# Expert rows by one-hot products instead of gathers: two transformer blocks with a mixture of experts on one core

## The chip, the cores and the metric

The kernel runs on one core of a Trainium2 chip. The metric is the device time of one execution in microseconds (us). A core has TensorE (PE, matmuls; its weight loads are listed as PEld), VectorE (DVE), ScalarE (ACT), GpSimd (POOL) and SyncE (SP), each with its own instruction queue, and 16 DMA engines that all queues share. The queues wait for each other on semaphores only. SBUF is the memory of 128 partitions on the core, PSUM the eight banks (2 KB for each partition) that TensorE writes to, HBM (DRAM) the memory outside.

## The reference, cut to what matters

A first pair of blocks (attention variants and convolution FFNs) feeds a second pair, whose mixers are a latent attention (layer 0) and a short convolution (layer 1). Each layer of the second pair ends in a mixture of experts on 256 tokens of width 1024, all in float32:

```python
g_prob = jax.nn.softmax(hf @ w_group, axis=-1)                 # 4 groups
g_sel = jnp.argmax(g_prob + b_group, axis=-1)
e_prob = jax.nn.softmax(chosen group's 8 logits)               # 32 experts in all
_, top_idx = lax.top_k(e_prob + e_bias, 2)                     # 2 experts of that group
top_w = top_w / sum(top_w) * g_w
y[token] = sum over its 2 experts: w * (silu(x @ w_gate[e]) * (x @ w_up[e])) @ w_down[e]
x = x + g2 * y
```

That is 512 assignments of a token to an expert in each layer. An expert's three matrices (1024 x 512, 1024 x 512, 512 x 1024) are 6.29 MB, so the 32 experts of a layer are 201 MB.

## The kernel before, in words

**Routing.** VectorE and TensorE work out for each token its two experts and a slot for each assignment. Slots are cut into 48 blocks (`NB`) of 32 slots; each block belongs to one expert, every expert has at least one block, and the blocks that no expert needs are spread over the experts by share (`rest`, `pad_i`). Three blocks make a round, so there are 16 rounds (`ROUNDS`) of 96 slots (`ROWS`). The end of the routing (`route`, L2331 to L2366) makes from the slot numbers `dst_f` two one-hot factors (`onA`, `onB`), multiplies them on TensorE, and reads off for each slot of each round the token (`token_i`), the row in which its result goes (`yrow_i`) and its weight (`slot_w`). `tab_i` tells each engine which of three buffers a block's expert lies in and how many loads must have landed; `need_i` tells SP when a buffer is free.

**Rows of a round.** ScalarE stores the normalized tokens `fN` to `f_rows` in DRAM (L1730, L1735). POOL gathers the 96 rows of a round from there into `xe` by an indirect DMA (L2764); indices of empty slots are out of bounds and are skipped. TensorE turns `xe` (eight transposes, L1208), ScalarE copies them out of PSUM into `xeT` (L1665).

**A round** (`turn` on TensorE and VectorE, the loop over `b` on ScalarE). Eight quarters of gate and up products, then four of down products, each with three column tiles of 32 columns on TensorE at once, one for each block (L1216 twice, L1218 once). One block's weights are read where they were loaded; those of the two others are first copied quarter by quarter into `side`, by VectorE (L2400) and ScalarE (L1684). VectorE's `landed` and `tail_landed` wait for the loads at quarters 0 and 2 of each matrix and tell ScalarE (`half_landed`). ScalarE's silu (L1672) and VectorE's product with `slot_w` (L2421) give `hm`; four transposes (L1245) and two copies (L2427) turn it, and the down products follow. VectorE multiplies the result by the gate row `gb2` into `ym` (`rows_out`, L2408, after the second copy of the next round), and POOL scatters `ym` to `y_rows` in DRAM by an indirect DMA (L2775). TensorE and VectorE run their rounds in hardware loops, so VectorE reads its four values of `tab_i` at the start of each round (L2412, L2413).

**Weights.** SP loads the experts in order into the three buffers, in half-matrices of 1 MB (`load_experts`, L767): gate of expert e, down of e-1, up of e. Each half waits until the rounds that use the old expert in that buffer are done with it (`need_i` against `quarter_done`). The first three experts are loaded before the rounds.

**After the rounds.** SP reads `y_rows` back (L812), two contributions to each token, and VectorE adds them to the residual (`combine`, L2448, L2449). For layer 1, VectorE (`row_diags`, L2213), TensorE (`row_pair`, two products of 128x128 by 128x512 a pair) and ScalarE (L1656) then spread three gate rows over the partitions. Squares (L1565), a root, transposes and the convolution's products (L843) follow in layer 0; the closing norm and the store follow in layer 1.

## Time and profile before

| what | value |
|---|---|
| time, 3 runs | median 2247.94 us (2244.13 to 2252.44) |
| the profiled execution | time 2246.04 us, span 2244.2 us |
| mean granted TensorE clock | 0.932 of full |
| rounds of layer 0 | first products at 1066.5 us, last result written at 1555.4 us |
| rounds of layer 1 | first products at 1730.6 us, last result written at 2220.8 us |

The span is the time between the first and the last record of the profiled execution; its own time has 1.8 us more around it. Times inside the profile are counted from the span's start. Busy shares are those of an engine's own instructions; an engine that waits for a semaphore is idle.

### The profile page before, as it was taken

The page shows a single profiled execution, that of the slowest core. Times are in us where ns is not written, and L with a number is a line of the kernel's source. Part 1 is how long each engine was busy: PE and PEld are TensorE (multiplying, and loading weights), DVE is VectorE, ACT ScalarE, POOL GpSimd, SP SyncE. Part 2 cuts the span into 40 slices and gives each one's busy share as a digit, 9 for nine tenths or more (in the row PEclk, how much of TensorE's full clock was granted, in tenths as well). Part 3 has the DMA queues.
Part 4 walks back from the last instruction along what each step waited for, and adds up shares of the span by engine and source line. Part 5 has one row for each costly group of instructions (what it writes and reads, how often), then busy time and mean ns, then how long its engine had stood idle before and what let it go on. Part 6 is the DMA issues. An engine that isn't in the chain of part 4 may idle for free.

```text
span 2244.2 us, 29502 instructions
## 1 busy us (share of the span) xinstructions
PE 1929.4 (86%) x9453; PEld 1085.2 (48%) x9454; DVE 956.4 (43%) x2077; ACT 665.8 (30%) x1053; POOL 100.0 (4%) x133
## 2 busy tenths in 40 slices
PE   8878999999999999997976887777897967877885
PEld 4534777745577775554432433333764423323332
DVE  2273888312478534444432432334224423323333
ACT  1142000012400002132543543444102534434443
POOL 2000000000000000000000000000000000000000
PEclk9869999999899999998998998999997988888998
DMA  8502898433179543305899999996645999999994
GB/s 282 201 6 99 325 343 312 178 141 143 66 277 358 197 167 132 124 31 207 334 421 383 360 412 407 407 416 260 258 160 221 385 421 379 415 421 389 411 394 166
DMA packets 84611, 617.69 MB, mean 275 GB/s; under 512 B 16289, under 2 KB 16609, under 8 KB 21809
## 3 DMA queue, kind: packets, MB, share of 16 engines
q1 hardware_dynamic: 68912, 544.70, 61.3%
q0 software_dynamic: 14752, 69.77, 8.3%
q10 hardware_dynamic: 864, 2.19, 0.2%
q8 instruction: 44, 0.72, 0.1%
q14 instruction: 39, 0.31, 0.0%
HBM read 621.84 MB, written 19.92 MB: 286 GB/s over the span
## 4 chain that ended last, share of the span: by engine, by line
PE 67%; DMA 19%; DVE 5%; issue 3%; ACT 3%; DVEq 2%; SPq 1%; ACTq 0%; POOLq 0%
PE ps L843 25%; PE ps L1216 15%; PE ps L1053 14%; DMA big<-in_w_up 7%; PE ps L1065 7%; DMA big<-in_w_down 5%; DMA big<-in_w_gate 5%; PE ps L1218 3%; PE ps L857 2%; ACT big L1684 2%; DVEq L2413 1%; DVE hT L2421 1%; PE ps L1245 1%; DMA c_res<-f_rows,big 1%; PE ps L1208 1%
## 5 line engine op out<-in xcount | busy, mean ns | idle before, releaser
L1216 PE MATMUL ps<-big,hT 128*32 128x512 f32 x3072 | 723.5, 627 | 144.0 <-ACT big L1684 140.5
L1218 PE MATMUL ps<-big,hT 128*32 x1536 | 722.3, 627 | 0.0
L1684 ACT COPY big<-big 128x1024 f32 x384 | 395.0, 1046 | 526.2 <-PE ps L1218 267.1
L2400 DVE TENSOR_SCALAR big<-big 128x1024 f32 x384 | 263.0, 696 | 623.0 <-PE ps L1218 375.6
L1216 PEld LDWEIGHTS ps<-big,hT 128*32 128x32 f32 x3072 | 200.5, 114 | 541.3 <-DVE big L2400 276.0
L1053 PE MATMUL ps<-hT,big 128*128 128x256 f32 x1408 | 311.1, 379 | 0.0
L843 PE MATMUL ps<-big,hT 128*128 128x512 f32 (+4 forms) x792 | 299.7, 537 | 4.8 <-DMA big<-in_dense 2.5
L1053 PEld LDWEIGHTS ps<-hT,big 128*128 128x128 f32 x1408 | 266.7, 190 | 49.0 <-issue 14.8
L843 PEld LDWEIGHTS ps<-big,hT 128*128 128x128 f32 x792 | 144.4, 195 | 149.3 <-issue 139.7
L843 PE MATMUL ps<-big 64*30 64x256 f32 (+14 forms) x704 | 161.4, 512 | 30.7 <-DVE big L2350 8.3
L1218 PEld LDWEIGHTS ps<-big,hT 128*32 128x32 f32 x1536 | 164.8, 114 | 6.1 <-issue 0.9
L1065 PE MATMUL ps<-big 128*128 128x512 f32 x352 | 159.2, 595 | 0.4 <-DVE big L2163 0.4
L2173 DVE SCALAR_TENSOR_TENSOR big<-big,s_ccol 128x512 f32<-128x512 f32 x196 | 147.4, 752 | 7.0
L1648 ACT ACTIVATE big<-big 128x256 f32<-128x256 f32 x44 | 18.3, 417 | 363.8 <-DVE big L2155 363.8
L843 PEld LDWEIGHTS ps<-big 64*128 64x128 f32 (+8 forms) x704 | 81.7, 196 | 90.3 <-issue 63.1
L843 PE MATMUL ps<-hT,big 128*128 128x256 f32 (+1 forms) x480 | 112.8, 398 | 1.9 <-ACT hT L1897 1.9
L843 PEld LDWEIGHTS ps<-hT,big 128*128 128x128 f32 x480 | 92.4, 193 | 22.7 <-issue 10.7
L1065 PEld LDWEIGHTS ps<-big 128*128 128x128 f32 x352 | 66.1, 190 | 72.9 <-issue 69.0
L2137 DVE TENSOR_TENSOR big<-ps,big 128x512 f32<-128x512 f32 x44 | 30.4, 690 | 119.5 <-PE ps L1053 117.5
L1245 PE MATMUL ps<-c_ident,hT 96*128 96x96 f32 x128 | 29.5, 318 | 50.4 <-DVE hT L2421 50.4
L857 PE MATMUL ps<-c_ident,big 128*128 128x128 f32 (+4 forms) x349 | 57.4, 301 | 17.6 <-DVE big L2085 10.9
L2764 POOL DMA_INDIRECT c_res<-f_rows,big x32 | 32.5, 1014 | 715.4 <-PE ps L1208 486.7
(333 smaller groups left out, 1176.2 us busy)
## 6 DMA issues: line engine op xcount, KB each, us to landing
big<-in_w_down SPq DMA_DIRECT2D x128, 1024.0 KB
big<-in_w_gate SPq DMA_DIRECT2D x128, 1024.0 KB, 12.1
big<-in_w_up SPq DMA_DIRECT2D x128, 1024.0 KB, 12.9
big<-in_dense SPq DMA_DIRECT2D x52, 1536.0 KB, 8.3
big<-in_dense POOLq DMA_DIRECT2D x28, 2048.0 KB, 9.9
big<-in_dense SPq DMA_DIRECT2D x21, 2048.0 KB, 8.3
big<-in_dense SPq DMA_DIRECT2D x5, 1024.0 KB, 7.5
big<-y_rows SPq DMA_DIRECT2D x4, 1024.0 KB, 6.2
```

The lines of the kernel that those rows point to most:

```text
L843: ins = nc.tensor.matmul(out, lhsT, rhs, start=start, stop=stop)
L857: ins = nc.tensor.transpose(out, rows, const["ident"][0:k, 0:k])
L1053: ins = nc.tensor.matmul(ps[:, t % 2, f * S:(f + 1) * S], w[:, k, f * P:(f + 1) * P], hT[:, k, S:2 * S], start=k == 0, stop=k == KT - 1)
L1065: ins = nc.tensor.matmul(ps[:, 4 + 2 * c + h, :], gT[:, t % 2, c * P:(c + 1) * P], w[:, h * BW:(h + 1) * BW], start=t == 0, stop=t == FT - 1)
L1216: nc.tensor.matmul(ps[g * SLOTS:(g + 1) * SLOTS, bank, :], xT[:, k, g * SLOTS:(g + 1) * SLOTS], side[:, g - 1, quarter % 2, at:at + BW], s ...
L1218: return nc.tensor.matmul(ps[0:SLOTS, bank, :], xT[:, k, 0:SLOTS], experts3[:, bass.ds(here, 1), kind * CH + row:kind * CH + row + BW] .re ...
L1245: ins = nc.tensor.transpose(ps[:, 4 + 3 * h, k * ROWS:(k + 1) * ROWS], rows, const["ident"][0:ROWS, 0:ROWS])
L1684: nc.scalar.copy(side[:, 1, quarter % 2, :], experts3[:, bass.ds(there, 1), lo:lo + QW] .rearrange("p a n -> p (a n)")).then_inc(s["side2_ ...
L2137: tt(U[:, par, :, 2:S + 2], ps[:, par, :].rearrange("p (a b) -> p a b", a=2), token_scale, mult)\
L2173: ins = stt(acc, mod_w[j % 2][:, k, :], ccols[:, k, col:col + 1], acc, mult, add)
L2400: ts(side[:, 0, quarter % 2, :], experts3[:, bass.ds(there, 1), lo:lo + QW].rearrange("p a n -> p (a n)"), 1.0, None, mult).then_inc(s["si ...
L2764: nc.gpsimd.indirect_dma_start(out=xe, out_offset=None, in_=f_rows[:, :], in_offset=bass.IndirectOffsetOnAxis(ap=token_i[:, b:b + 1], axis=0),
```

## The change

It rewrites how a round gets its rows and gives its results back, and moves some work around it.

- **Rows by products.** `fN` stays in SBUF. VectorE writes for each round a one-hot matrix of tokens by slots (`first_pick`, `second_pick`: two `tensor_scalar` and two `scalar_tensor_tensor` of 128x96), and TensorE multiplies it with the tokens (`rows_of`: two banks, each two float32 products of 128x96 by 128x512). ScalarE and VectorE copy one half each out of PSUM into `xe` (`row_half`), and the eight transposes (`rows_T`) follow, now between the second and the third quarter of the down products of the round before. `f_rows`, its stores and the gathers are gone.
- **Results in slot order.** The slot weight is no longer multiplied into `hm`. ScalarE stores all 96 rows of `ym` to their place in `y_rows` by a plain DMA on its own queue (`store`, after the fourth copy of the next round). While the last round runs, POOL fetches each token's two rows by four indirect DMAs (`fetch`), and VectorE adds them with the token's weight. The last round's results are not stored: a weighted one-hot matrix (`last_picks`, `turn_last`, `hot`) spreads them by four products, and VectorE adds these last. The rows of the last round in `y_rows` are zeroed once, by two DMAs on POOL in the first FFN.
- **VectorE's rounds unrolled.** The values of the next round's `tab_i` are read in the middle of the round, two before the copies of the turned hidden rows and two after them. The ninth copy comes ahead of those copies too.
- **Routing.** The products of `onA` and `onB` and what leads to them are gone; `past` is made earlier, from a reduction, and `row_half` of round 0 stands ahead of `need_i` and `tab_i`. TensorE and ScalarE wait for the end of the routing only after round 0's transposes.
- **Layer 1's gate rows** are spread during the first three steps of the convolution, which has six PSUM banks in place of eight.

The spreading of the spare blocks, the loads of weights and their order are as before. The diff, cut to its core:

```diff
-                pe.wait_ge(g2["act_evac"].sem, g2["act_evac"].end)
-                for q in range(2 * TC):
-                    mm(ps[:, 6, 0:3 * ROUNDS], onA[:, q, :], onB[:, q, :, :], q == 0, q == 2 * TC - 1,
...
-                def rows_T(b, h, first=False):
-                    if h == 0:
-                        pe.wait_ge(s["rows_gathered"].sem, s["rows_gathered"].at(b * 16 + 16))
...
+                def rows_of(b, first=False):
+
+                    pe.wait_ge(s["pick_ready"].sem, s["pick_ready"].at(b * TC + TC))
...
+                    for h in range(2):
+                        for t in range(T):
+                            ins = nc.tensor.matmul(ps[0:ROWS, h, :], onehot[:, t, :], fN[:, t, h * BW:(h + 1) * BW],
+                                                   start=t == 0, stop=t == T - 1)
+                        ins.then_inc(s["rows_ready"].sem, 1)
...
+                def rows_T(b):
+
...
+                    for h in range(2):
+                        for k in range(4):
+                            rows = xe[0:ROWS, :].rearrange("t (p k) -> t k p", k=KT)[:, 4 * h + k, :]
+                            ins = nc.tensor.transpose(ps[:, h, k * ROWS:(k + 1) * ROWS], rows,
...
+                    if more:
+                        rows_of(b + 1)
+                    else:
+                        turn_last()
                     for h in range(2):
-                        if more:
-                            rows_T(b + 1, h)
...
                     for k in range(FFK):
+                        if k == 2 and more:
+                            rows_T(b + 1)
...
-                rows_T(0, 0, first=True)
-                rows_T(0, 1, first=True)
+                rows_of(0, first=True)
+                rows_T(0)
+                after(pe, "ent" + name[-1], "route" + name[-1], "g2_" + name[-1])
...
+                for c in range(T):
+                    for h in range(2):
+                        if c == 0:
+                            pe.wait_ge(m["last_ready"].sem, m["last_ready"].at(h + 1))
+                        mm(ps[:, 2 * c + h, :], hot[0:ROWS, c, :], ym[0:ROWS, h * BW:(h + 1) * BW], True, True,
...
+                if t < 3:
+                    if t:
+                        g = st["g1_1"]["gate_copied"]
+                        pe.wait_ge(g.sem, g.at(2 * t))
+                    row_pair("g1_1", t, CONV_BANKS)
...
+                def store(b):
+                    act.wait_ge(s["y_ready"].sem, s["y_ready"].at(b + 1))
+                    act.dma_start(rows[b * ROWS:(b + 1) * ROWS, :], ym[0:ROWS, :]).then_inc(s["y_stored"].sem, 16)
...
+                row_half(0)
+                rows_T(0)
+                after(act, "route" + name[-1])
                 there = third(0)
...
-                    for j in range(2, 6):
+                    for j in range(2, 4):
+                        copy(b, there, j)
+                    if b:
+                        store(b - 1)
+                    for j in range(4, 6):
...
+                    here = there
+                    if b + 1 < ROUNDS:
+                        row_half(b + 1)
+                        there = third(b + 1)
+                    for j in range(10, 12):
+                        copy(b, here, j)
...
-                act.wait_ge(e["z_done"].sem, e["z_done"].end)
-                act.dma_start(f_rows[0:P, :], fN[:, 0, :]).then_inc(e["f_stored"].sem, 16)
...
-                L(nc.vector.tensor_copy(dst_i, dst_f))
...
-                L(tt(onA, iota(4, P), wide(q_f, P), ALU.is_equal))
-                for x in range(3):
-                    ins = tt(onB[:, :, x, :], eqB, wide(vals[:, :, x], ROUNDS), mult)
...
+                L(stt(rel, iota(4, ROUNDS), -float(ROWS), wide(dst_f, ROUNDS), mult, add))
+                m = st["moe" + tag]
+                first_pick(m, 0)
+                second_pick(m, 0)
+                row_half(m, 0)
+                nc.vector.tensor_copy(row_i, dst_f)
...
+            def first_pick(s, b):
+
+                for t in range(TC):
+                    ts(onehot[:, t, :], const["iota"][:, 0:ROWS], rel[:, t, b:b + 1], None, ALU.is_equal)\
...
+                for t in range(TC):
+                    v.wait_ge(s["pick_step"].sem, s["pick_step"].at(b * TC + (t + 1)))
+                    stt(onehot[:, t, :], const["iota"][:, 0:ROWS], rel[:, TC + t, b:b + 1], onehot[:, t, :],
...
-                def turn(b, first=False, second=False):
-                    there = v.value_load(tab_i[0:1, 0, bass.ds(b * WIDE + 1, 1)], min_val=0, max_val=BPE - 1)
...
-                            rows_out(b - 1, second)
+                            rows_out(b - 1)
+                        if j == 3 and not last:
+                            v.wait_ge(s["rows_ready"].sem, s["rows_ready"].at(b * 2 + 2))
+                            first_pick(s, b + 1)
+                        if j == 4 and not last:
+                            second_pick(s, b + 1)
+                        if j == 4 and last:
+                            last_picks()
...
-                    stt(hm[0:ROWS, :], sgm[0:ROWS, :], slot_w[0:ROWS, bass.ds(b, 1)], ps[0:ROWS, 3, :], mult, mult)\
-                        .then_inc(s["hidden_done"].sem, 1)
+                    tt(hm[0:ROWS, :], sgm[0:ROWS, :], ps[0:ROWS, 3, :], mult).then_inc(s["hidden_done"].sem, 1)
+                    copy(b, there, loads, 9, first)
+                    if not last:
+                        then, ahead = second(b + 1), [loads_of(b + 1, 0)]
...
+                    if not last:
+                        row_half(s, b + 1)
+                        ahead += [loads_of(b + 1, q) for q in range(1, BPE)]
+                        following = then, ahead
...
-                turn(0, True)
-                after(v, "g2_" + name[-1])
-                turn(1, False, True)
-                with v.Fori(2, ROUNDS) as b:
-                    turn(b)
...
+                values = second(0), [loads_of(0, q) for q in range(BPE)]
+                for b in range(ROUNDS):
...
+                    values = turn(b, *values)
+                v.wait_ge(m["last_turned"].sem, m["last_turned"].end)
+                nc.vector.tensor_copy(hot[0:ROWS, :, :], ps[0:ROWS, 0, 0:T * P].rearrange("p (c n) -> p c n", c=T))\
...
                 for c in range(T):
-                    v.wait_ge(s[f"y_fetched_{c}"].sem, s[f"y_fetched_{c}"].end)
-                    for h in range(2):
-                        cols = slice(h * BW, (h + 1) * BW)
...
-                        link(v, tt(out, out, y01[:, c, 0, cols], add))
-                        tt(out, out, y01[:, c, 1, cols], add).then_inc(s["combined"].sem, 1)
+                    v.wait_ge(m[f"y_fetched_{c}"].sem, m[f"y_fetched_{c}"].end)
+                    for k in range(2):
+                        link(v, stt(lat(c), y01[c][:, k, :], tok_w[:, k * T + c:k * T + c + 1], lat(c), mult, add))
...
+                for h in range(2):
+                    cols = slice(h * BW, (h + 1) * BW)
+                    tt(ym[0:ROWS, cols], ps[0:ROWS, 5 + h, :], gb2[0:ROWS, 0, cols], mult).then_inc(m["last_ready"].sem, 1)
+                for i, (out, c, h) in enumerate(parts):
+                    v.wait_ge(m["last_spread"].sem, m["last_spread"].at(i + 1))
+                    tt(out, out, ps[:, 2 * c + h, :], add).then_inc(m["combined"].sem, 1)
...
+            row_diags("g1_1", 1)
...
-                    nc.gpsimd.indirect_dma_start(
-                        out=xe, out_offset=None, in_=f_rows[:, :],
-                        in_offset=bass.IndirectOffsetOnAxis(ap=token_i[:, b:b + 1], axis=0),
-                        bounds_check=S - 1, oob_is_err=False).then_inc(s["rows_gathered"].sem, 16)
...
-                    nc.gpsimd.indirect_dma_start(
-                        out=y_rows[:, :], out_offset=bass.IndirectOffsetOnAxis(ap=yrow_i[:, b:b + 1], axis=0),
-                        in_=ym, in_offset=None, bounds_check=2 * S - 1, oob_is_err=False)\
...
+                        nc.gpsimd.indirect_dma_start(
+                            out=y01[c][:, k, :], out_offset=None, in_=y_rows[layer][:, :],
+                            in_offset=bass.IndirectOffsetOnAxis(ap=row_i[:, q:q + 1], axis=0),
...
+                pool.dma_start(y_rows[l][(ROUNDS - 1) * ROWS:ROUNDS * ROWS, :], zeros[0:ROWS, :])\
```

## Rows read from the trace of the kernel before

**Rows 1.** The page: GB/s moved in each of 40 slices.
```profile
GB/s 282 201 6 99 325 343 312 178 141 143 66 277 358 197 167 132 124 31 207 334 421 383 360 412 407 407 416 260 258 160 221 385 421 379 415 421 389 411 394 166
```

**Rows 2.** Stretches: length, busy time and count by engine; TensorE clock, DMA share, GB/s.
```profile
1071.70:1100.00 28.30, 26.36 (x182) 12.07 (x179) 12.03 (x18) 17.09 (x18) 2.01 (x2) 1.00 0.89 329
1100.00:1540.00 440.00, 347.50 (x2204) 153.70 (x2201) 149.22 (x226) 193.17 (x213) 27.70 (x27) 0.93 0.99 402
...
1577.80:1662.70 84.90, 84.88 (x384) 74.10 (x384) 16.24 (x39) 8.00 (x15) 0.00 (x0) 0.98 0.57 217
...
1760.00:2195.00 435.00, 344.01 (x2173) 150.72 (x2167) 146.00 (x221) 189.60 (x208) 27.13 (x27) 0.91 1.00 405
...
1278.00:1290.00 12.00, 11.13 (x78) 5.83 (x81) 6.19 (x9) 7.81 (x9) 1.01 (x1) 1.00 0.57 190
```

**Rows 3.** Groups by line in layer 0's rounds: busy us, mean ns, idle before them.
```profile
L1216 PE MATMUL ps<-big,hT 128*32 128x512 f32 x1536 | 361.1, 625 | 70.0 <-ACT big L1684 69.6 <-DVE hT L2427 0.3
...
L1208 PE MATMUL ps<-c_ident,c_res 96*128 96x96 f32 x126 | 21.2, 296 | 0.0
...
L1245 PE MATMUL ps<-c_ident,hT 96*128 96x96 f32 x64 | 14.7, 317 | 27.3 <-DVE hT L2421 27.3
```

**Rows 4.** Timeline (start, us): two rows_out, and the first product between rounds.
```profile
1093.08 1.21 DVE L2408 TENSOR_TENSOR c_res<-ps,hT 96x1024 f32<-96x1024 f32 x1
...
1117.67 1.21 DVE L2408 TENSOR_TENSOR c_res<-ps,hT 96x1024 f32<-96x1024 f32 x1
...
1117.47 0.62 PE L1216 MATMUL ps<-big,hT 128*32 128x512 f32 x2 [1.35 <-ACT big L1684]
```

**Rows 5.** Timeline of SP and TensorE in a later round: two issues of down weights, one wait.
```profile
1231.39 0.92 SPq L767 DMA_DIRECT2D big<-in_w_down  x2
...
1262.66 0.84 SPq L767 DMA_DIRECT2D big<-in_w_down  x2
...
1243.10 0.48 PE L1245 MATMUL ps<-c_ident,hT 96*128 96x96 f32 x2 [3.53 <-DVE hT L2421]
```

**Rows 6.** Chain that ended last, two pieces of the down products behind that wait.
```profile
1245.55 0.85 PE ps L1216 x2
...
1248.01 0.42 PE ps L1216 x2
```

**Rows 7.** Timeline of POOL, DVE and PE at the start of layer 0's rounds.
```profile
1056.10 1.06 POOL L2764 DMA_INDIRECT c_res<-f_rows,big  x1 [49.73 <-DVE big L2366]
...
1059.68 0.69 DVE L2400 TENSOR_SCALAR big<-big 128x1024 f32 x1 [3.62 <-issue]
...
1063.40 1.51 PE L1208 MATMUL ps<-c_ident,c_res 96*128 96x96 f32 x8 [7.79 <-DMA c_res<-f_rows,big]
...
1066.52 1.07 PE L1216 MATMUL ps<-big,hT 128*32 128x512 f32 x2 [1.60 <-ACT big L1684]
```

**Rows 8.** Chain: eight records of a 128x512 product, four float32 products, at full clock.
```profile
1026.19 3.44 PE ps L843 x8
```

**Rows 9.** One line, 1100 to 1540 us: DVE's loads of table values, min/median/max ns.
```profile
L2413 DVEq TENSOR_LOAD <-big x42: 297/304/324, 1113.8 to 1525.7; - x42
```

**Rows 10.** Timeline: last rows_out and last square, of layer 0 and of layer 1.
```profile
1554.14 1.22 DVE L2408 TENSOR_TENSOR c_res<-ps,hT 96x1024 f32<-96x1024 f32 x1 [2.63 <-PE ps L1218]
...
1572.51 0.19 ACT L1565 ACTIVATION_READ_ACCUMULATOR big<-x_res 128x1 f32 x1
...
2219.53 1.22 DVE L2408 TENSOR_TENSOR c_res<-ps,hT 96x1024 f32<-96x1024 f32 x1 [2.63 <-PE ps L1218]
...
2236.91 0.19 ACT L1565 ACTIVATION_READ_ACCUMULATOR big<-x_res 128x1 f32 x1
```

**Rows 11.** Groups by form: a product-and-add of 128x1024 and an addition of 128x512.
```profile
L2449 DVE TENSOR_TENSOR x_res<-x_res,big 128x512 f32<-128x512 f32 x8 | 5.5, 692 | 0.3
...
L2244 DVE SCALAR_TENSOR_TENSOR big<-x_res,rstd_x,c_res 128x1024 f32<-128x1024 f32 x2 | 2.6, 1277 | 0.0
```

**Rows 12.** One tensor, y_rows: DMAs from issue to landing, us.
```profile
DMA to landing us min/median/max: 3.1/8.2/9.1
```

288 lines of the change are left out of this document (146 added, 142 removed).

## The prediction, made before the changed kernel ran

> **What bounds the kernel now.** I read the slices of the page first [rows 1]. The two stretches near 400 GB/s are the rounds of the experts, 2 x 490 us of 2244, and all but a few edits lie in them or at their ends. The highest slice is 421 GB/s; I take it as the rate of a full stream. The stretches [rows 2] then show how near to it the rounds are: 402 and 405 GB/s, with TensorE busy 79% of the time. So the weights' stream nearly sets the pace: two experts a round, 12.58 MB, plus 0.26 MB of gathered and scattered rows (only the 512 real ones of a layer move) is 12.84 MB, or 30.5 us at 421. But the stream has holes: 1071.7 to 1100 at 329, and 1278 to 1290 at 190 GB/s [rows 2]. In each layer they are worth some 25 us, and who makes them decides this change.
>
> Three kinds of round can be told apart.
> - *TensorE sets it.* Two results stand 24.6 us apart [rows 4]. That is 48 groups of 0.43 us (two records of L1216 a group, 1536 in 16 rounds [rows 3]), so 20.6, and 4.0 of turning rows, waits and a gap of 1.35 at the round's start, where the side copies wait for VectorE, which reads its table there [rows 4].
> - *A loop sets it.* Two issues of down weights stand 31.3 us apart [rows 5]. A down load can't be issued until the gate products of its round let the gate load ahead of it in SP's queue go; VectorE's ninth copy waits for the landing, and the hidden product is behind that copy in VectorE's queue. TensorE stands idle for 3.53 us in front of the hidden transposes [rows 5]. Of the 16 waits in layer 0, which sum to 27.3 [rows 3], 7 are of 2.7 to 3.6 us; layer 1 has 6 of 2.5 to 3.6.
> - *The stream sets it*: the rest, 8 in each layer.
>
> **Part 1, the pick products and where they stand.** A round gets four float32 products of 512 columns, 3.44 us at full clock [rows 8], after the up products. Its eight transposes were 1.3 us beside them (21.2 for 126 [rows 3]) and are now 1.4 inside the down products. VectorE's ninth copy (0.69) and two table reads come ahead of the copies of the turned hidden rows. A read's load alone takes 0.30 us [rows 9]; four reads with the landing waits took 3.62 [rows 7]; I take 0.5 a read (0.3 to 0.9). The gap at the round's start goes, as the table is read early.
>
> In a round that TensorE sets: 3.44 hides the hidden product, the copy and the reads; the down products start 4.4 us after the last up product in place of 2.15, so +2.2; transposes +1.4; gap -1.4; sum +2.2 us, 26.8 in all. I count one such round in layer 0 whose length reaches the end (the one in front of the hole at 1278), and in layer 1 two, one of them half covered: +2.2 and +3.3. The first three rounds are as long, but three experts were there before them and the stream runs full behind them: their lengthening costs only the first down load's release, +1.0 in each layer (0 to 2.2).
>
> In a loop round the products stand in the 3.53 us in which TensorE waits for the down weights to land, so they cost nothing; without that wait they would cost 2.2 as above. After the wait: the copy and the reads ahead, less the four transposes that leave, +0.7; transposes +1.4; gap -1.5; and TensorE's clock. The four groups behind the wait took 0.85 to 1.0 us and the later ones 0.42 [rows 6]: the lower level of 1.2 GHz, then 2.4. With the products in the wait the idle time is under 1.7 us, shorter than waits after which groups of full speed stand in this trace, so -1.7. Sum -1.1 (+0.6 if the clock still falls). But each round now stores all 96 rows, 0.39 MB in place of 0.26, so the stream's own floor is 12.98 MB, 30.8 us. From 31.3 to 30.8 is -0.5: 7 rounds -3.5, 6 rounds -3.0. Bounds: +0.6 and -0.5 a round.
>
> In a stream round the 0.13 MB costs 0.3 us: +2.4 in each layer (0 if the store fills holes).
>
> **Part 2, the start of the rounds.** Now: the gather starts at 1056.1, the transposes at 1063.4, the first product at 1066.5 [rows 7]. After: `dst_f` is ready near 1051.0 (five tiny operations ahead of the picks, 0.2 each, in place of seven and two products), picks 1052.1. The four products take 3.44 at full clock or 6.88 at the lower level, at which the first group at 1066.5 ran (1.07 [rows 7]); I take 5.5, near the colder end, as the clock recovered 2.9 us into that work: 1057.6. Half row copy 0.7, need and table 1.2, VectorE's reads and landing waits 3.6 as before, ScalarE's side copy 1.05: 1064.3. So -2.2 in each layer (-4.3 to -0.8). POOL and ScalarE lose their gather and two stores here; nobody waited for those stores.
>
> **Part 3, the end.** From the last down product (0.1 us ahead of `rows_out`) to the last square: 1572.7 less 1554.0 is 18.7 us in layer 0, and 2237.1 less 2219.4 is 17.7 in layer 1 [rows 10]. After it, counted from that product: VectorE is free 2.7 us before it; `hot` and the gains to -1.9; four `scalar_tensor_tensor` of 1024 columns at 1.28 plus 0.03 [rows 11] to +3.3; two halves of the gated result at 0.65 to +4.6. TensorE has idled 4 us by the first half, so I take its first two products at 1.72 (the lower level) and the others between: 5.8, 7.5, 8.6, 9.5; the last addition of 0.69 [rows 11] ends at 10.2 and its square at 11.2. That is -7.5 and -6.5 (-9.4 and -8.4 with a warm clock). It needs the fetched rows by -1.9. The store of round 14 is issued some 4.8 us into a last round of 23, at -18; with the usual 8.2 us [rows 12] it lands at -10; four gathers of 1.0 us on POOL go out by -6 and land within 3.1 (idle queues) to 8.2. The first token tile is there in time, the second up to 2 us late: 0 to +3 us.
>
> The Trainium skill's page "DMA: Bandwidth & Descriptors" (section "Anatomy of one DMA — SWDGE (gpsimd) path") gives a DMA from GpSimd 2.0 us plus its bytes at 436 GB/s; by that estimate a 512 KB gather lands 3.2 us after its issue, and all four are there by -2. The trace's shortest, 3.1 us for up to 393 KB, agrees.
>
> **Part 4, moved work.** The six gate-row products of layer 1, 12 records of 0.43, go from TensorE's idle time before the convolution into a stretch in which TensorE is busy 84.88 of 84.90 us [rows 2]: +5.2, all in layer 0's tail. VectorE's diagonals there (3 x 1.2) and ScalarE's copies have that stretch's slack. Zeroing rows in the first FFN holds POOL's second modulation load some 10 us; VectorE needs it near 240 and it would land near 242, with 5 us of slack before TensorE cares: 0 (0 to 2).
>
> **The sum.** Layer 0: -2.2 + 1.0 - 3.5 + 2.4 + 2.2 - 7.5 + 5.2 = -2.4. Layer 1: -2.2 + 1.0 - 3.0 + 2.4 + 3.3 - 6.5 = -5.0. Together -7.4 us on the profiled execution's 2246.0, so 2238.6; the median shown, 2247.9, is 1.9 above that one, which would make it 2240.5. I predict 2240.
>
> **The rivals.**
> - *The holes close.* The loop's slack of 1.1 and the round gap let SP's releases come earlier everywhere. Layer 0's 440 us at 402 [rows 2] hold 20 us of holes, layer 1's 435 at 405 hold 16. If a third of them goes, 12 us, the time is 2228. For it: the gap of 1.35 stands in every round. Against: the largest hole comes after a round that gets longer. Chance 0.24.
> - *The picks reach the down loads (slower).* If the wait in front of the hidden transposes is not theirs to fill, because VectorE's longer way behind it or a late pick pushes the down products, each loop round grows by 2.2 in place of shrinking by 0.5: 13 x 2.7 = +35, so 2274. It decides from a loop round of 31.3 + 0.1 = 31.4 us on: -7.4 is gone there, and at 32.2 the kernel is slower by over 0.5%. For it: the loop runs through those very products. Against: 3.53 us of wait for 3.44 of work. Chance 0.12.
> - *The end is late and the rest cancels (no change).* POOL's gathers stand beside VectorE's side copies of the last round, 0.69 in each 1.72 us. If a copy holds POOL up, four gathers take 7 us in place of 4, the second tile is 3 to 5 us late in each layer, and with the start's lesser bound (-0.8) the sum is near +3: 2249. Against: 32 scatters in this kernel's rounds took 0.97 to 1.5 us on POOL, mostly 1.0, amid the same copies. Chance 0.16. The Trainium skill's page "SBUF — State Buffer" (section "SBUF: two separate sides") states such a lock: while VectorE runs a copy in its two-port mode, GpSimd can't write its descriptors. By the same rule the store gains from ScalarE's queue.
> - *My forecast*, 2232 to 2247: 0.48.
>
> **How the numbers follow.** 0.5% of the median is 11 us, about what a measurement of this kernel can tell from no change: below 2236.7 is faster, above 2259 slower. The first rival and 0.14 of the forecast's range lie below: 0.38. The slower rival gives 0.11 above. The rest is 0.51. The range leaves out most of the slower rival and 0.08 at the fast end: 2222 to 2256.
>
> **What the changed profile should show.** Pick products of 3.4 us behind each round's up products, and in loop rounds under 1.7 us of idle time behind them; the groups after them at 0.43. Rounds of about 26.8 us where there were 24.6, and of 30.8 where there were 31.3. No gap at a round's start. First product 2 us sooner after the routing. From the last down product to the last square 11 us. A convolution stretch of 90 us. The forecast fails if the loop rounds are longer than before, if the landing of the fetched rows ends the tail, or if the stream's holes shrink or grow by more than 10 us.

## The result, and the profile after

| | before | after |
|---|---|---|
| median of 6 runs | 2247.08 us (2241.96 to 2252.44) | 2228.42 us (2224.86 to 2235.16) |
| ratio, 95% interval | | 0.992 (0.990 to 0.995) |
| the profiled execution | 2246.04 us, span 2244.2 | 2226.99 us, span 2225.2 |
| mean granted TensorE clock | 0.932 | 0.950 |

The change gives 18.7 us, two and a half times the forecast's 7.4, and the time of the first rival (2228). I go through the trace as the prediction does. First the page's slices, GB/s, against [rows 1]:

```profile
GB/s 284 194 15 79 333 351 315 185 134 171 39 251 363 237 148 132 151 38 160 255 423 421 411 374 410 401 419 361 238 193 202 322 422 422 410 423 418 407 413 218
```

Then stretches of the changed kernel (length, busy time and count by engine, clock, DMA share, GB/s), against [rows 2]:

```profile
1071.70:1100.00 28.30, 27.28 (x172) 12.04 (x168) 12.09 (x22) 15.56 (x17) 0.00 (x0) 1.00 0.77 264
1100.00:1540.00 440.00, 391.06 (x2349) 167.03 (x2346) 170.82 (x304) 202.82 (x229) 0.73 (x1) 0.95 0.99 409
1570.60:1660.20 89.60, 89.60 (x396) 76.12 (x396) 19.82 (x43) 11.45 (x21) 0.00 (x0) 0.98 0.51 191
1750.00:2182.00 432.00, 381.54 (x2302) 158.80 (x2299) 166.70 (x294) 198.94 (x225) 0.00 (x0) 0.95 1.01 414
1278.00:1290.00 12.00, 12.00 (x87) 3.82 (x81) 6.71 (x12) 7.81 (x8) 0.00 (x0) 1.00 0.53 194
```

The rounds' streams went from 402 and 405 to 409 and 414 GB/s, and TensorE is busy 89% of the first and 88% of the second. The hole near 1278 is still there (194 for 190); the smaller ones went. I count a hole as the shortfall from 421 in 2 us slices under 405 GB/s, between the start and the end of a layer's stream: 17.8 us in layer 0 and 16.2 in layer 1 before, 12.0 and 4.2 after. The bounds move such a number by one or two us: with fixed ones, 1110 to 1530 and 1770 to 2160 us, the sums are 19.3 and 15.1 before and 13.4 and 5.5 after.

The waits of TensorE from 1100 to 1540 us (us in total, times, longest), of the kernel before:

```profile
PE ps L1216 <- ACT big L1684: 66.4, 24, 15.4
PE ps L1245 <- DVE hT L2421: 26.0, 14, 3.5
```

and of the changed one:

```profile
PE ps L1221 <- ACT big L1705: 45.5, 15, 14.3
PE ps L1221 <- DVE hT L2478: 2.9, 14, 0.2
PE ps L1252 <- DVE hT L2472: 0.5, 2, 0.4
```

The wait in front of the hidden transposes (now L1252) fell from 26.0 to 0.5 us, as forecast: the pick products fill it. A round's inside in the timeline: two results 26.6 us apart (26.8 forecast), then pick products, hidden transposes without a wait, and the first down products at full clock.

```profile
1098.65 1.21 DVE L2448 TENSOR_TENSOR c_res<-ps,hT 96x1024 f32<-96x1024 f32 x1
1125.24 1.21 DVE L2448 TENSOR_TENSOR c_res<-ps,hT 96x1024 f32<-96x1024 f32 x1
...
1241.01 3.67 PE L1194 MATMUL ps<-big,hT 128*96 128x512 f32 x8
1244.52 0.60 PE L1252 MATMUL ps<-c_ident,hT 96*128 96x96 f32 x4
1245.33 0.62 PE L1221 MATMUL ps<-big,hT 128*32 128x512 f32 x2 [0.21 <-DVE hT L2478]
```

The start of layer 0's rounds, against [rows 7]: the first pick products take 6.30 us (5.5 forecast), and then the table and VectorE's reads.

```profile
1052.16 0.38 PE L837 MATMUL ps<-c_ones,big 32*128 32x32 f32 x2
...
1056.13 6.30 PE L1194 MATMUL ps<-big,hT 128*96 128x512 f32 x8 [1.46 <-DVE hT L2406]
...
1067.57 1.30 DVE L2440 TENSOR_SCALAR big<-big 128x1024 f32 x2 [3.49 <-issue]
1068.69 1.07 PE L1221 MATMUL ps<-big,hT 128*32 128x512 f32 x2 [4.29 <-ACT big L1705]
```

The end of layer 0, against [rows 10]: the fetched rows are added without a wait, TensorE idles 4.17 us until VectorE made the halves (L2521), and the last square is at 1565.1.

```profile
1552.09 5.25 DVE L2516 SCALAR_TENSOR_TENSOR x_res<-big,x_res 128x1024 f32<-128x1024 f32 x4
...
1553.44 0.59 PE L1223 MATMUL ps<-big,hT 128*32 x1
...
1557.37 1.28 DVE L2521 TENSOR_TENSOR c_res<-ps,hT 96x512 f32<-96x512 f32 x2
1558.20 6.16 PE L837 MATMUL ps<-c_res,hT 96*128 96x512 f32 x8 [4.17 <-DVE c_res L2521]
...
1565.12 0.63 ACT L1586 ACTIVATE big<-x_res 128x512 f32<-128x512 f32 x1
```

Cut at the same instructions in both traces, the 19.0 us of span come from here:

| stretch | before | after | difference | forecast |
|---|---|---|---|---|
| to the routing's 32x32 product, layer 0 | 1048.16 | 1052.16 | +4.0 | 0 |
| to the first expert product | 18.36 | 16.53 | -1.8 | -2.2 |
| to the last down product | 486.99 | 484.75 | **-2.2** | +2.1 |
| to the convolution's first product | 24.31 | 17.11 | -7.2 | -7.5 |
| the convolution's first part | 87.52 | 92.32 | +4.8 | +5.2 |
| to that 32x32 product, layer 1 | 47.10 | 43.72 | -3.4 | 0 |
| to the first expert product | 18.11 | 16.81 | -1.3 | -2.2 |
| to the last down product | 488.35 | 483.38 | **-5.0** | +3.7 |
| to the end of the span | 25.30 | 18.42 | -6.9 | -6.5 |

The two stretches with a forecast of 0 differ by +4.0 and -3.4 and cancel. The first holds small parts of the change (the zeroing, the moved routing work), but it also varies by itself: 1044.3 to 1049.9 us in the five traces of the kernel before and its variants, 1045.3 to 1053.3 in the nine of the changed kernel and its variants. In the second, the same work had a granted clock of 0.89 before and of 1.00 after. Start, end and convolution came within 0.9 us of their terms each. The rounds are the miss: -7.2 us where +5.8 stood.

The -7.2 is the difference of two single traces. Other traces with the same rounds bound it. From the first expert product to the result of a layer's fifteenth round, layer 0 took 461.1 and 461.6 us with the rounds before (run 7 and the kernel before) and 458.4, 459.1 and 461.3 with the changed ones (run 11, the changed kernel and run 10). Layer 1 took 466.0 before and 461.9 and 463.9 after. So the rounds gained 0 to 3 us in layer 0 and 2 to 4 in layer 1 up to there, and not +2.1 and +3.7.

### The profile page after: what moved, and what is told of

Same layout as the page of the kernel before. It is cut to its first block, busy times and chain, and to the rows that moved or that the text cites. A ratio compares the mean times of both kernels' runs of the same rounds, so it can differ in the third digit from the quotient of the medians.

```text
span 2225.2 us, 29562 instructions
## 1 busy us (share of the span) xinstructions
PE 2026.7 (91%) x9701; PEld 1106.8 (50%) x9702; DVE 1002.5 (45%) x2221; ACT 682.3 (31%) x1085; POOL 46.6 (2%) x79
## 4 chain that ended last, share of the span: by engine, by line
PE 77%; DMA 13%; DVE 5%; ACT 2%; issue 2%; SPq 1%; DVEq 0%; ACTq 0%
PE ps L837 26%; PE ps L1221 20%; PE ps L1047 14%; DMA big<-in_w_up 7%; PE ps L1059 7%; DMA big<-in_w_gate 4%; PE ps L1194 4%; PE ps L1223 3%; PE ps L851 2%; DMA big<-in_w_down 1%; ACT big L1705 1%; PE ps L1205 1%; DMA big<-in_dense 1%; DVE x_res L2516 0%; DVE big L2100 0%
## 5 line engine op out<-in xcount | busy, mean ns | idle before, releaser
L1221 PE MATMUL ps<-big,hT 128*32 128x512 f32 x3072 | 703.8, 612 | 109.4 <-ACT big L1705 102.4
L1223 PE MATMUL ps<-big,hT 128*32 x1536 | 703.3, 612 | 0.0
L1221 PEld LDWEIGHTS ps<-big,hT 128*32 128x32 f32 x3072 | 187.8, 112 | 484.0 <-issue 255.9
L837 PE MATMUL ps<-big 64*30 64x256 f32 (+12 forms) x684 | 155.8, 519 | 24.6 <-issue 5.5
L1223 PEld LDWEIGHTS ps<-big,hT 128*32 128x32 f32 x1536 | 159.6, 112 | 5.6
L1194 PE MATMUL ps<-big,hT 128*96 128x512 f32 x256 | 123.2, 626 | 2.6 <-DVE hT L2406 2.6
L837 PEld LDWEIGHTS ps<-big 128*128 128x128 f32 (+7 forms) x684 | 77.7, 195 | 83.6 <-issue 65.9
L1194 PEld LDWEIGHTS ps<-big,hT 128*96 128x96 f32 x256 | 40.8, 169 | 82.9 <-issue 79.9
```

The source lines that it names most:

```text
L837: ins = nc.tensor.matmul(out, lhsT, rhs, start=start, stop=stop)
L1194: ins = nc.tensor.matmul(ps[0:ROWS, h, :], onehot[:, t, :], fN[:, t, h * BW:(h + 1) * BW], start=t == 0, stop=t == T - 1)
L1221: nc.tensor.matmul(ps[g * SLOTS:(g + 1) * SLOTS, bank, :], xT[:, k, g * SLOTS:(g + 1) * SLOTS], side[:, g - 1, quarter % 2, at:at + BW], s ...
L1223: return nc.tensor.matmul(ps[0:SLOTS, bank, :], xT[:, k, 0:SLOTS], experts3[:, bass.ds(here, 1), kind * CH + row:kind * CH + row + BW] .re ...
```

## The experiments

All times are medians against runs of the kernel before on the same chip; the changed kernel has 0.992.

**1. VectorE's reads late.**

```diff
-                def turn(b, there, loads):
+                def turn(b):
...
+                    there, loads = second(b), [loads_of(b, q) for q in range(BPE)]
```

> The changed kernel, with VectorE's four table reads of a round at the round's start again, as in the kernel before. Measured so far: the change gives 2228.4 us for 2247.1 (ratio 0.992), and the holes in the middle of the weights' stream (2 us slices under 405 GB/s, their shortfall from 421 summed, without the start and the end of a layer) went from 17.8 to 12.0 us in layer 0 and from 16.2 to 4.2 in layer 1. Theory A, the gap: the gap of 1.35 to 1.5 us in front of a round's first products made TensorE release each expert's slot late, and the holes close because it is gone. Then the gap comes back in nearly every round and most of the 18 us of holes with it: 10 to 18 us slower than the changed kernel, about 2242, ratio 0.998. Theory B, the queue: the holes close because GpSimd's gathers and scatters (0.26 MB a round) are out of the stream's way. Then only rounds that TensorE sets pay, some 3 of them uncovered at 1.4 us: +4 us, 2232, ratio 0.994. Theory C, the wait: they close because the pick products stand where TensorE waited 3.5 us and its clock stays up; then as B.

2227.3 us, ratio 0.991 (0.989 to 0.992): nothing. Theory A isn't tried by it, though. Rounds that TensorE sets took 26.7 and 26.4 us (26.6 and 26.4 in the changed kernel): with the rounds written out, the reads fit into VectorE's idle time even there.

**2. Gathers of GpSimd added, and 3. the same bytes by a plain store.**

```diff
+                for b in range(13):
+                    pool.wait_ge(s["y_ready"].sem, s["y_ready"].at(b + 1))
...
+                    for k in range(2):
+                        nc.gpsimd.indirect_dma_start(
+                            out=c_res[96:128, k, :], out_offset=None, in_=dram["w_down"].rearrange("e p (r d) -> (e p r) d", d=D),
+                            in_offset=bass.IndirectOffsetOnAxis(ap=row_i[0:32, k:k + 1], axis=0),
...
```

> The changed kernel, and in each of the first 13 rounds GpSimd gathers twice 32 rows of 4 KB (0.26 MB, as much as the gather and scatter of a round in the kernel before) from the down weights into partitions that nothing reads. Work is added; the result stays. Theory B (GpSimd's gathers make the holes): the holes of 12 us a layer open again on top of the bytes: 2 x 12 plus the price of 3.4 MB a layer (8.1 us at 421 GB/s), 2260 or more, ratio over 1.005, and well above the run that stores the same bytes with a plain store. Theory A and C: the bytes alone, 8 us a layer at most where the stream has no room, so 2236 to 2244, and the same as the run with the plain store.

```diff
+                    act.dma_start(more[b * ROWS:b * ROWS + 64, :], ym[0:64, :]).then_inc(s["y_stored"].sem, 16)
```

> The changed kernel, and each round's store is followed by a second store of 64 rows (0.26 MB) to rows that nobody reads, from the same queue. It prices the stored bytes. If the stream sets nearly every round now (middle of layer 1 at 416 GB/s of 421), 0.26 MB costs 0.62 us in each of 15 rounds: +9 us a layer, 2246, ratio 1.000. If, as I forecast, only 8 rounds a layer are the stream's and a loop sets 6 or 7: +5 a layer, 2238, ratio 0.996. If stores fill holes: 2229.

2254.6 us, ratio 1.004 (1.002 to 1.005), with the gathers; 2241.9, ratio 0.997 (0.996 to 0.999), with the store. The gathers moved 13 rounds' worth a layer and the store 15, yet they cost 26 us against 13.5. Holes: 15.3 and 10.6 us in the two layers with the gathers, 11.2 and 4.9 with the store (12.0 and 4.2 without either). The gathers' time lies between its two expectations (2236 to 2244, and 2260 or more), and the holes grew by 3.3 and 6.4 us where 12 each were expected; the store's lies between 2238 and 2246. The stretches 1100 to 1540 and 1760 to 2180 us with the gathers:

```profile
1100.00:1540.00 440.00, 385.49 (x2276) 160.98 (x2272) 164.76 (x289) 196.77 (x223) 24.28 (x24) 0.93 1.00 406
1760.00:2180.00 420.00, 358.16 (x2126) 149.01 (x2120) 154.81 (x273) 183.44 (x206) 26.74 (x26) 0.93 1.01 409
```

and with the plain store:

```profile
1100.00:1540.00 440.00, 390.34 (x2316) 166.79 (x2312) 168.03 (x296) 200.24 (x226) 0.00 (x0) 0.94 1.00 411
1760.00:2180.00 420.00, 364.42 (x2177) 153.81 (x2174) 158.78 (x281) 188.15 (x212) 0.00 (x0) 0.94 1.01 415
```

So a byte costs about twice as much as a gather of GpSimd's than as a plain store of ScalarE's. This pair differs in more than the form, though: the gathers load, from the down weights' memory and beside the weights' loads, and the stores write. Runs 5 to 7 keep the direction.

**4. Fewer stored bytes.**

```diff
-                    act.dma_start(rows[b * ROWS:(b + 1) * ROWS, :], ym[0:ROWS, :]).then_inc(s["y_stored"].sem, 16)
+                    act.dma_start(rows[b * ROWS:b * ROWS + 32, :], ym[0:32, :]).then_inc(s["y_stored"].sem, 16)
```

> The changed kernel with 32 of the 96 rows stored in a round, and the rows fetched at the end taken from the down weights, so that the combined rows are wrong: the output leaves the stored results out. 0.26 MB a round less than the changed kernel, 0.13 less than the kernel before. The stream sets the rounds: 0.62 us in 15 rounds, -9 us a layer, 2210, ratio 0.983, unless rounds that TensorE sets (26.4 us) take over. Loops set half of them: -5 a layer, 2218, ratio 0.987. Bytes cost nothing: 2228.

2216.3 us, ratio 0.986 (0.984 to 0.988): -12 us for -0.26 MB a round; run 3 gave +13.5 for +0.26, so about 13 for either. At 421 GB/s the 7.9 MB of 30 rounds are 18.7 us, so two thirds of a byte's stream time is paid, and the change's own 0.13 MB a round costs some 6.4 us. (Layer 1 routes other tokens in this run.)

**5 and 6. The kernel before with plain transfers**, issued by GpSimd and by ScalarE:

```diff
-                    nc.gpsimd.indirect_dma_start(
-                        out=xe, out_offset=None, in_=f_rows[:, :],
...
+                    pool.dma_start(xe[0:32, :], f_rows[14 * b:14 * b + 32, :]).then_inc(s["rows_gathered"].sem, 16)
...
-                    nc.gpsimd.indirect_dma_start(
-                        out=y_rows[:, :], out_offset=bass.IndirectOffsetOnAxis(ap=yrow_i[:, b:b + 1], axis=0),
...
+                    pool.dma_start(y_rows[32 * b:32 * b + 32, :], ym[0:32, :]).then_inc(s["y_stored"].sem, 16)
```

> The kernel before, with the gather and the scatter of a round replaced by plain loads and stores of 32 rows from the same place in GpSimd's program (0.13 MB each, as much as the real rows of a round); the picked rows are left out, so the output is wrong and layer 1 routes other tokens. Known now: reading the table late costs the changed kernel nothing (0.9905), and two gathers a round cost it 13 us more than a plain store of the same bytes. Theory B1, the gathers' form (addresses read from a table, a descriptor for each row): the holes close here as in the change, 8 to 14 us faster than before, ratio 0.994 to 0.996. Theory B2, GpSimd's queue itself: plain transfers in it make the same holes, ratio 1.000. Theory C, the pick products fill TensorE's wait: 1.000 too.

> The same, and the plain loads and stores are issued by ScalarE, the load behind its copies of the turned rows and the store as in the changed kernel; GpSimd issues nothing in the rounds. Theory B1: as the run beside it, 0.994 to 0.996. Theory B2: 0.994 to 0.996 here and 1.000 there. Theory C: 1.000 in both.

2216.9 and 2215.9 us, ratio 0.986 (0.985 to 0.988) for both. It is not GpSimd's queue but the form of the transfer, and more than any theory had: 30 and 31 us. The two forms differ in the DMA view of 1100 to 1540 us. Of the kernel before:

```profile
DMA packets 27790, 176.93 MB, mean 402 GB/s; under 512 B 5745, under 2 KB 5745, under 8 KB 6650
...
q0 software_dynamic: 4000, 3.72, 2.5%
...
big<-in_w_gate SPq DMA_DIRECT2D x53, 1024.0 KB, 13.0
y_rows<-c_res,big POOLq DMA_INDIRECT x14, 8.3
```

and of the kernel with plain transfers in GpSimd's program:

```profile
DMA packets 25122, 176.99 MB, mean 402 GB/s; under 512 B 3088, under 2 KB 3088, under 8 KB 3952
...
q0 software_dynamic: 1296, 3.54, 2.3%
...
big<-in_w_gate SPq DMA_DIRECT2D x53, 1024.0 KB, 11.1
y_rows<-c_res POOLq DMA_DIRECT2D x14, 128.0 KB, 5.4
```

GpSimd's queue (q0) moved nearly the same bytes in 4000 packets where the plain transfers need 1296. Over all queues there are 2657 packets under 512 B fewer (3088 for 5745): about 100 for each of the 27 gathers and scatters, near the 96 of 128 partitions that hold no real row on the mean (512 rows in 16 rounds are 32). The transfers themselves land sooner in plain form (5.4 us after their issue for 8.3), but in neither trace does TensorE or VectorE wait for one of them between 1100 and 1540 us, so it is not that a round's rows came late. Halves of gate weights landed 13.0 us after their issue and 11.1 without the indirect transfers; in ScalarE's version, as fast, it is 12.0, so this number alone carries nothing. In layer 0, whose routing is the same, the last result is written 7.3 us earlier. The Trainium skill's page "DMA: Bandwidth & Descriptors" (section "Specifications") asks for at least 512 B a transfer for the full rate, since the engine reads and writes back for less; the direction agrees.

That the small packets are the price is not shown. The time of the queue's packets differs little (2.5% of that of the 16 engines for 2.3%), and run 2 speaks against them as the only cause. Its gathers name 32 rows for 32 partitions, and the DMA view of the same stretch shows them without extra packets, 51 each (a plain transfer has 48):

```profile
q0 software_dynamic: 1234, 3.35, 2.2%
...
c_res<-in_w_down,big POOLq DMA_INDIRECT x24, 7.0
```

They cost 26 us all the same. The indirect form also reads its addresses from a table and its rows from scattered places; which of these holds the stream up, and how, no run here separates.

**7. The same in layer 1 alone**, so that the tokens' routing is kept:

```diff
+                    if name == "moe1":
+                        pool.dma_start(xe[0:32, :], f_rows[14 * b:14 * b + 32, :]).then_inc(s["rows_gathered"].sem, 16)
+                        return
...
+                    if name == "moe1":
+                        pool.dma_start(y_rows[32 * b:32 * b + 32, :], ym[0:32, :]).then_inc(s["y_stored"].sem, 16)
+                        continue
```

> The kernel before, with plain loads and stores of 32 rows in place of the gathers and scatters in layer 1 alone, so that layer 1 routes the same tokens as before (its own result is wrong: the picked rows are left out). With both layers plain it was 31 us; layer 0, whose routing is the same there, showed 7.3 us of it in its rounds. Theory B1: 7 to 15 us faster here, ratio 0.993 to 0.997. If most of the 31 came from other routing in layer 1: 0 to 3 us, ratio 0.999 to 1.000.

2232.7 us, ratio 0.994 (0.992 to 0.995): 14 us from the 32 transfers of one layer, as Theory B1 has it. Layer 1's stream from 1760 to 2180 us, before and in this run:

```profile
1760.00:2180.00 420.00, 329.53 (x2077) 144.53 (x2071) 140.56 (x212) 181.96 (x200) 27.13 (x27) 0.90 1.00 405
```

```profile
1760.00:2180.00 420.00, 336.40 (x2145) 150.13 (x2145) 144.25 (x220) 188.06 (x207) 12.73 (x26) 0.91 1.01 414
```

Its holes fell from 16.2 to 6.5 us, and first to last result took 450.9 us for 461.4, so 10.5 of the 14 us show in the rounds.

**8. VectorE's rounds written out, alone.**

```diff
-                with v.Fori(2, ROUNDS) as b:
-                    turn(b)
...
+                for b in range(ROUNDS):
...
+                    values = turn(b, *values, b == 0, b == 1)
```

> The kernel before, with VectorE's rounds written out and its four table reads of the next round made ahead of the copies 10 and 11: that part of the change alone. In the run with late reads the changed kernel had no gap at the round's start either, so the gap was not tried there; here it is. Theory A (the gap makes the holes): 1.4 us less in each TensorE-set round and each loop round, 10 to 18 us faster, ratio 0.993 to 0.995. Theory B1 (the gathers' form makes them: plain transfers in their place gave 0.986): the stream is where it was, 0 to 4 us faster, 0.998 to 1.000.

2243.3 us, ratio 0.998 (0.997 to 0.999). The gap at the round's start went from 1.35 to 0.37 us and TensorE-set rounds from 24.6 to 23.5; holes 15.0 and 15.3 us. Worth 3.4 us: Theory A falls as the main cause.

**9. The pick products twice, and 10. none in layer 1.**

```diff
+                    for time in range(1 if first else 2):
+                        for h in range(2):
+                            for t in range(T):
...
+                            if first or time:
+                                ins.then_inc(s["rows_ready"].sem, 1)
```

> The changed kernel with the four pick products of rounds 1 to 15 made twice, 3.44 us more of TensorE in each round at full clock. If the stream sets the rounds (30.8 us and more against 26.4 that TensorE needs), rounds of 29.8 still fit: 0 to 8 us slower than the changed kernel (the round before the hole near 1280 us and one or two in layer 1), 2228 to 2236. If a loop through these products sets some 7 rounds of a layer, as I forecast of the kernel before: 13 x 3.4 = +45, 2273. This also tells Theory C: if room in TensorE is what closed the holes, they open again here, as wide as before (+12).

2275.6 us, ratio 1.014 (1.012 to 1.016): 47 us. My expectation of 0 to 8 was wrong and the other right. Rounds that TensorE sets grew to 29.8 us, as they must. Those of 30.9 to 32.7 us in layer 0 became 30.2 to 35.3, five of the eight 34.0 or more, and the holes 29.4 and 21.3 us. TensorE's waits from 1100 to 1540 us shrank from 45.5 to 21.1:

```profile
PE ps L1223 <- ACT big L1707: 21.1, 9, 3.6
```

A round that waits for a landing is not saved by that wait: the load it waits for was itself issued late, behind products that the added 3.44 us had pushed. SP's issues in the twelfth round of layer 0 show it, first in the changed kernel:

```profile
1423.31 0.94 SPq L771 DMA_DIRECT2D big<-in_w_gate  x2
1429.87 4.97 SPq L771 DMA_DIRECT2D big<-in_w_down  x2
```

and then with the products made twice:

```profile
1434.72 0.94 SPq L771 DMA_DIRECT2D big<-in_w_gate  x2
1444.72 0.33 SPq L771 DMA_DIRECT2D big<-in_w_down  x1
```

The down load follows the gate loads by 6.6 us and by 10.0.

And the run without them in layer 1:

```diff
+                    if name == "moe1" and not first:
+                        for h in range(2):
+                            nc.tensor.matmul(ps[0:ROWS, h, 0:32], onehot[:, 0, :], fN[:, 0, 0:32], start=True, stop=True)\
+                                .then_inc(s["rows_ready"].sem, 1)
+                        return
```

> The changed kernel with the four pick products of 512 columns of a round cut to two of 32 columns in rounds 1 to 15 of layer 1, so that its picked rows are left out and its result is wrong; 3.3 us of TensorE's time go from each of 15 rounds. Making them twice cost 47 us in both layers, 24 a layer. If the products cost as much the first time: 24 us faster than the changed kernel, 2204, ratio 0.981. If they stand in a wait as I forecast, or the stream (4 us of holes left in the middle of layer 1) is what is left: 3 to 8 us faster, 2220 to 2225, ratio 0.989 to 0.991.

2224.4 us, ratio 0.991 (0.989 to 0.993): 4 us, within the uncertainty, since this interval and the changed kernel's overlap. Of 50 us of TensorE's work taken out of layer 1 almost nothing comes back; it turns into waits (us in total, times, longest; 1760 to 2180 us), where the changed kernel has 47.2 and 0.3:

```profile
PE ps L1226 <- ACT big L1710: 54.4, 12, 15.4
PE ps L1257 <- DVE hT L2477: 17.9, 14, 3.4
```

So the pick products as they stand cost little: some 4 us in layer 1, not clear of nothing, and if layer 0 is alike 0 to 8 in both. As much again costs half its length (47 us for 30 x 3.44): the changed kernel stands near the edge where the stream's pace passes to TensorE's.

**11. Another order at the end.**

```diff
+                fetched(0)
                 v.wait_ge(done.sem, done.end)
...
                     tt(ym[0:ROWS, cols], ps[0:ROWS, 5 + h, :], gb2[0:ROWS, 0, cols], mult).then_inc(m["last_ready"].sem, 1)
+                fetched(1)
```

> The changed kernel with another order at the end of a layer: VectorE makes the two halves of the last round's gated rows behind the fetched rows of the first token tile, and the fetched rows of the second tile behind them, while TensorE spreads. In the changed kernel's layer 0 TensorE waits 4.2 us for the halves (until 1558.2) and VectorE then waits 1.6, 1.0 and 0.9 us for the products. The halves come 2.6 us earlier; the fetched rows of the second tile (2.6 us) stand where VectorE waits now. So 2.5 to 3 us less in each layer, -5 to -6, 2223, ratio 0.9897. Rival: the fetched rows land late, and their wait now stands ahead of everything: no change, or slower by 2.

2221.7 us, ratio 0.989 (0.987 to 0.991), the best kernel of this study, and 6.7 us under the changed one. In its timeline the halves are at 1555.35, TensorE idles 1.53 us in place of 4.17, and the eight records of the spread take 3.67 us in place of 6.16:

```profile
1552.70 2.60 DVE L2516 SCALAR_TENSOR_TENSOR x_res<-big,x_res 128x1024 f32<-128x1024 f32 x2
...
1555.35 1.28 DVE L2523 TENSOR_TENSOR c_res<-ps,hT 96x512 f32<-96x512 f32 x2
...
1556.18 3.67 PE L837 MATMUL ps<-c_res,hT 96*128 96x512 f32 x8 [1.53 <-DVE c_res L2523]
...
1559.17 2.48 DVE L2527 TENSOR_TENSOR x_res<-x_res,ps 128x512 f32<-128x512 f32 x4
```

The last square ends 7.8 us after the last down product in layer 0 and 7.4 in layer 1 (11.8 and 10.6 in the changed kernel): -7.2 in all. I had left out the clock's share: the granted clock was 0.50 from 1558.2 to 1561.0 us and 0.63 from there to 1564.0 in the changed kernel, and is 1.00 from 1556.2 to 1559.9 here.

**12. The pick products before the up products' third quarter.**

```diff
+                            if more and (kind, quarter) == (1, 2):
+                                rows_of(b + 1)
                             both_copied(b, 4 * kind + quarter)
...
-                    if more:
-                        rows_of(b + 1)
-                    else:
+                    if not more:
                         turn_last()
```

> The kernel with the other order at the end, and the pick products of the next round moved from behind the up products to before their third quarter, where TensorE waits 2.7 to 3.7 us for the second half of the up weights in about every second stream round of the changed kernel. The products are then behind the release of half the up weights only and out of the way between the last up product and the down products. If they cost time where they stand: 4 to 10 us less than the kernel with the other order (2221.7), 2212 to 2218, ratio 0.984 to 0.987. If the stream alone sets these rounds: no change, 0.989. Worse if they push the up products past the landing: 0.991.

2260.5 us, ratio 1.006 (1.004 to 1.008): 39 us slower than run 11, outside all three expectations. Two things show, in the waits from 1100 to 1540 us:

```profile
PE ps L1221 <- ACT big L1705: 39.0, 10, 8.7
PE ps L1252 <- DVE hT L2472: 12.2, 14, 0.9
PE ps L1221 <- DVE hT L2478: 6.0, 14, 0.7
```

With nothing between the last up product and the hidden transposes TensorE waits for VectorE in every round, 0.9 us in front of the transposes and 0.4 behind them (12.2 and 6.0 us in all for 0.5 and 2.9 in run 11), and TensorE-set rounds are 27.8 us for 26.4. And the other rounds grew to 31.5 to 36 us with holes of 30.1 and 20.5 us. My reading, not tried apart, is that only every second of them had had its wait at that place, while the products now stand ahead of the release of half the up weights in all of them.

## Why the prediction was right and wrong, point by point

- **Inside its range, wrong in its middle.** 2228 lies between 2222 and 2256; the likeliest was 2240. It is inside because the range was wide enough to take in the first rival, not because the sum was right. That rival, "the holes close", gave 2228 and named the right symptom (10 to 20 us of holes gone) with causes that the runs don't bear out: the round gap is worth 3.4 us, not 12. That its time is met to a microsecond is luck.
- **The step that failed** is in the first part of the text, "12.58 MB, plus 0.26 MB of gathered and scattered rows", and goes through the sum: a transfer was priced by its bytes alone, so that taking 64 indirect transfers out was worth nothing and storing 0.13 MB more cost +2.4 a layer. Measured in the kernel before, their form was worth 14 us in layer 1 (run 7, 10.5 of them in its rounds) and 7 in layer 0 (run 5's trace). In the changed kernel it was not measured by itself.
- **The stored bytes** were a term of +4.8 and cost about +6.4 (runs 3 and 4): the mechanism is right, the size was somewhat small.
- **The pick products.** That they fill the wait in front of the hidden transposes is right (26.0 to 0.5 us), and +2.2 a TensorE-set round nearly so (24.6 to 26.5, +1.9). That they cost nothing in a loop round is nearly right as they stand (run 10), but the argument behind it, a wait of 3.53 us as room to fill, is wrong in general: run 9 filled waits of 2 to 4 us and paid half, run 12 moved work into one and lost 39.
- **The loop rounds** were to go from 31.3 to 30.8. They stand at 30.9 to 32.7 in layer 0 and 30.8 to 32.2 in layer 1, so the -3.5 and -3.0 are not there as such; what went are rounds of 33.5 to 33.7 (two in layer 0, one in layer 1). The first four rounds of layer 0 took 123.0 us for 122.8: three longer ones are given back in the fourth (40.0 for 47.0), as the text had it, to 0.2 us of its +1.0. TensorE's clock stayed up, 0.95 for 0.93 and 0.91 in the stretches [rows 2].
- **The second and third rivals.** The slower one did not come, but its place, the loop through these products, is where run 9 lost 47 us. POOL's four gathers took 1.05 to 1.41 us each, 5.7 in all with the gaps between them: they did slow down, as that rival has it, but VectorE's additions of the fetched rows did not wait for them. The rows landed 4.6 to 6.4 us after their issue. The estimate by the Trainium skill's page "DMA: Bandwidth & Descriptors" (section "Anatomy of one DMA — SWDGE (gpsimd) path") was 3.2; with the last issue at 1543.6 and the need at 1552.1 neither decides.
- **Start, end, convolution**: -3.1, -14.1 and +4.8 for -4.4, -14.0 and +5.2. At the start the four products took 6.30 us for 5.5: nearly all at the lower clock. The zeroing was to cost 0: TensorE's waits from 180 to 300 us are the same in both traces (1.7, 0.7 and 0.3 us).
- **The account of the rounds.** By their parts, the form -10.5 and -7, the gap -3.4, the bytes +6.4 and the pick products 0 to +8 give -6.5 to -14.5, where the traces show -7.2 with some 3 us of scatter. The parts come from other neighbours and need not add; what of the form's price the fuller stream of the changed kernel would have hidden anyway stays open, as does the larger gain of runs 5 and 6 (30 and 31 us, of which other routing in layer 1 may be a part).

## What to carry to other kernels

Don't price an indirect transfer by its bytes alone. Its packets in the DMA view are a first hint; what it costs shows when you move the same bytes in plain form, even in a run that leaves the right rows out. A wait of TensorE for a load is not free room: if the awaited load is released by TensorE itself, work put in front of the release makes the wait come back. And order the last step so that TensorE's input is made first: here that also kept its clock up (run 11). Before you explain a few us between two traces, look at how much other traces of the same code differ.

## What the runs showed of the hardware

- A gather or scatter of 96 slots of which 32 hold a row sent about 100 packets under 512 B beside its rows. Plain transfers in place of 32 of them, in one layer of a kernel whose stream runs at 96% of its rate, gave 14 us (run 7).
- Gathers of 32 rows into 32 partitions sent no such packets (51 each), and still cost 26 us for 6.8 MB where plain stores cost 13.5 us for 7.9 MB (runs 2 and 3).
- Plain transfers of 0.13 MB cost the same in GpSimd's program and in ScalarE's (2216.9 and 2215.9 us).
- Eight records of 96x512 took 6.16 us behind 4.17 us of idle time (granted clock 0.50, then 0.63) and 3.67 us behind 1.53 us (1.00).
